# Both expert tables in one, with 8 KB rows gathered once per expert

## What is computed

```python
def peer_ffn(x, w_q, sub_keys, u, v):
    q = (x @ w_q).reshape(B, S, PEER_HEADS, 2, PEER_DK // 2)
    s = jnp.einsum('bshcd,cnd->bshcn', q, sub_keys)
    sv, si = lax.top_k(s, PEER_TOPK)
    ...
    best_s, pos = lax.top_k(cand_s, PEER_TOPK)
    e_idx = jnp.take_along_axis(cand_i, pos, axis=-1)
    gate = jax.nn.softmax(best_s, axis=-1)
    ...
        hid = jax.nn.gelu(jnp.einsum('td,ted->te', xt, u[et]), approximate=False)
        return jnp.einsum('te,ted->td', gt * hid, v[et])
```

## Time and profile before

| | |
|---|---|
| timed, median of 3 | 1822.17 us (1818.75 to 1827.27) |
| profiled execution, span from first to last instruction | 1995.1 us |
| PE, DVE, ACT, POOL busy | 1482.2, 1007.4, 342.9, 1016.4 us |
| gather queue | 536.94 MB, 71.5% of 16 DMA engines |

### The profile page before, as it was taken

One profiled execution on the slowest core, in us unless ns is written; L12 is line 12 of the kernel. 1 busy time (PEld: TensorE's weight loads), 2 busy tenths in 40 slices (PEclk: granted clock), 3 DMA queues, 4 the chain that ended last, 5 costly groups with the idle time before them and its releaser, 6 DMA issues.

```text
span 1995.1 us, 18642 instructions
## 1 busy us (share of the span) xinstructions
PE 1482.2 (74%) x4236; PEld 720.2 (36%) x4236; DVE 1007.4 (50%) x2400; ACT 342.9 (17%) x921; POOL 1016.4 (51%) x1197
## 2 busy tenths in 40 slices
PE   7997467777666877766889974577776777777677
PEld 5775233344322422222345552244432222222223
DVE  0226766666664544444122267666666645434442
ACT  1222111111111111111123221111110211111111
POOL 1111556655566466666400005555555666666663
PEclk8998688888898989999988887988888999998999
DMA  7764998999899799999812228989997999999996
GB/s 167 153 142 158 327 372 328 331 340 331 329 356 371 281 358 367 375 366 369 300 49 57 54 78 323 352 323 342 336 337 303 364 371 378 362 359 365 361 372 259
DMA packets 236447, 591.86 MB, mean 297 GB/s; under 512 B 59136, under 2 KB 100736, under 8 KB 236416
## 3 DMA queue, kind: packets, MB, share of 16 engines
q0 software_dynamic: 147456, 536.94, 71.5%
q1 hardware_dynamic: 88960, 54.57, 10.5%
HBM read 590.37 MB, written 1.05 MB: 296 GB/s over the span
## 4 chain that ended last, share of the span: by engine, by line
PE 22%; DVE 22%; issue 19%; POOL 13%; DMA 9%; another core or an unknown queue 5%; DVEq 3%; ACT 2%; POOLq 2%; SPq 1%; ACTq 1%
DVE u_rows L1124 9%; POOL v_rows L446 6%; POOL u_rows L439 6%; PE att L671 6%; DMA v_rows<-in_peer_v_dram,idx_v 5%; PE y L554 3%; DMA u_rows<-in_peer_u_dram,idx_u 3%; PE b_qk L565 3%; PE b_vo L574 1%; ACT shared L924 1%; PE att L527 1%; PE att L524 1%; DVE hit L1094 1%; DVE hit L1090 1%
## 5 line engine op out<-in xcount | busy, mean ns | idle before, releaser
L1124 DVE CUSTOM_DVE_ANT_0 u_rows<-y,u_rows 128x1024 f32<-128x1024 f32 x512 | 615.4, 1222 | 460.0 <-DMA u_rows<-in_peer_u_dram,idx_u 412.9
L446 POOL DMA_INDIRECT v_rows<-in_peer_v_dram,idx_v x512 | 483.8, 945 | 319.6 <-issue 147.0
L671 PE MATMUL att<-v_rows,shared 128*128 128x512 f32 x1024 | 510.8, 631 | 172.9 <-DMA v_rows<-in_peer_v_dram,idx_v 131.4
L439 POOL DMA_INDIRECT u_rows<-in_peer_u_dram,idx_u x512 | 485.6, 948 | 240.2 <-issue 158.6
L671 PE MATMUL y<-v_rows,shared 128*128 128x512 f32 x1024 | 493.1, 630 | 81.4 <-DMA v_rows<-in_peer_v_dram,idx_v 52.6
L671 PEld LDWEIGHTS att<-v_rows,shared 128*128 128x128 f32 x1024 | 184.3, 196 | 498.7 <-issue 454.3
L671 PEld LDWEIGHTS y<-v_rows,shared 128*128 128x128 f32 x1024 | 197.4, 202 | 368.3 <-issue 360.0
L646 PE MATMUL b_vo<-keysT,qT 128*128 128x128 f32 x128 | 28.4, 359 | 199.6 <-ACT qT L908 136.1
L924 ACT ACTIVATE shared<-ident,wts 128x128 f32<-128x128 f32 x512 | 154.2, 387 | 65.7 <-PE att L671 38.3
L919 ACT ACTIVATE act_hid<-hid 128x16 f32<-128x16 f32 x32 | 6.9, 216 | 819.9 <-issue 446.2
L632 PE MATMUL b_qk<-hT,w_pq 128*128 128x256 f32 x448 | 103.8, 392 | 3.8 <-DMA w_pq<-in_peer_w_q_dram 3.8
(11 more groups left out here) (158 smaller groups left out, 1068.1 us busy)
## 6 DMA issues: line engine op xcount, KB each, us to landing
w_pq<-in_peer_w_q_dram SPq DMA_DIRECT2D x16, 1024.0 KB
w_qk<-in_na_w_in_dram SPq DMA_DIRECT2D x16, 512.0 KB, 5.0
u_rows<-in_peer_u_dram,idx_u POOLq DMA_INDIRECT x512
v_rows<-in_peer_v_dram,idx_v POOLq DMA_INDIRECT x512
w_v<-in_na_w_in_dram SPq DMA_DIRECT2D x8, 512.0 KB, 3.8
shared<-in_na_rel_bias_dram SPq DMA_DIRECT2D x64, 64.0 KB, 4.6
w_o<-in_na_w_out_dram SPq DMA_DIRECT2D x8, 512.0 KB, 4.0
w_o<-in_mla_w_out_dram SPq DMA_DIRECT2D x8, 512.0 KB, 3.4
```

The lines of the kernel that those rows point to most:

```text
L439: pool.indirect_dma_start(u_rows[:, b, :], None, u_table, bass.IndirectOffsetOnAxis(ap=idx_u[:, half_no, b:b + 1], axis=0))\
L446: pool.indirect_dma_start(v_rows[:, b, :], None, v_table, bass.IndirectOffsetOnAxis(ap=idx_v[:, half_no, b:b + 1], axis=0))\
L671: last = nc.tensor.matmul(ffn[tile][:, c, :], diag[:, k, :], v_rows[:, b, c * 512:(c + 1) * 512], start=False, stop=stop and k == TOPK - 1)
L1124: V.tensor_tensor_reduce(out=rows, in0=px, in1=rows, scale=1.0, scalar=0.0, op0=ALU.mult, op1=ALU.add, accum_out=hid[:, k:k + 1])\
```

## The change

- The host lays u and v of an expert side by side in one table with rows of 8 KB (peer_uv). One gather brings both halves into one of 8 slots of uv_rows. The memory in SBUF is the same as that of the two rings before. A slot is free again after the expert's product on PE.
- v is no longer one group behind. In PE's loop the order is score_step(g+1), then add_experts(g).
- Weights are made for two experts at a time (SUB = 2): ACT's Gelu, DVE's product with the gates and ACT's two diagonals follow each pair of dots; DVE's part of a pair is placed after the first dot of the next pair. gate_exp moves into weigh, behind the fourth pair. One part of the choice of groups 0 and 7 is placed at other dots.
- POOL copies 16 indices at once, where it copied 8 for u and 8 for v.

```diff
+SUB = 2
+SUBS = TOPK // SUB
...
-        u_rows = sb("u_rows", [P, RING, D])
-        v_rows = sb("v_rows", [P, RING, D])
+        idx = sb("idx", [P, 2, TOPK], i32)
+        uv_rows = sb("uv_rows", [P, RING, 2, D])
...
+            def gather_group(layer, g, slot, heads=None):
+                n = layer * GROUPS + g
                 if heads is not None:
                     pool.wait_ge(s_top[0], layer * PH + heads)
                     pool.sem_inc(s_pool, 1)
+                nc.gpsimd.tensor_copy(idx[:, slot, :], expert_flat[:, ds(g * TOPK, TOPK)]).then_inc(s_ix, 1)
+                pool.wait_ge(s_ix, n + 1)
+                pool.sem_inc(s_pool, 1)
+                for k in range(TOPK):
+                    pool.wait_ge(s_acc, products_done(n * TOPK + k + 1 - RING))
+                    pool.sem_inc(s_pool, 1)
+                    pool.indirect_dma_start(uv_rows[:, k % RING, :, :].rearrange("p h d -> p (h d)"), None, uv_table,
+                                            bass.IndirectOffsetOnAxis(ap=idx[:, slot, k:k + 1], axis=0))\
+                        .then_inc(s_rows_in[k % RING], 16)
...
                     pe.wait_ge(s_diag, (base + g) * TOPK + k + 1)
-                    pe.wait_ge(s_vg[b], 16 * ((base + g) * 2 + k // RING + 1))
...
+                add_experts(layer, 0, 0)
                 with pe.Fori(1, PH - 1) as g:
                     score_step(layer, g + 1)
-                    add_experts(layer, 0, g - 1)
+                    add_experts(layer, 0, g)
                 score_step(layer, PH)
-                add_experts(layer, 0, PH - 2)
                 add_experts(layer, 0, PH - 1, stop=True)
+                add_experts(layer, 1, PH)
...
+                for s in range(SUBS):
+                    some = slice(s * SUB, (s + 1) * SUB)
+                    act.wait_ge(s_dot, (base + g) * TOPK + (s + 1) * SUB)
+                    nc.scalar.activation(act_hid[:, some], hid[:, some], ACT.Gelu).then_inc(s_gelu, 1)
+                    act.wait_ge(s_wts, (base + g) * SUBS + s + 1)
+                    for k in range(s * SUB, (s + 1) * SUB):
+                        if not first:
+                            act.wait_ge(s_acc, products_done((base + g - 1) * TOPK + k + 1))
+                        nc.scalar.activation(diag[:, k, :], ident[:, :], ACT.Copy, scale=wts[:, k:k + 1])\
+                          .then_inc(s_diag, 1)
+                    if s == 3 and choice is not None:
+                        gate_exp(layer, choice[0], choice[1])
...
                 with act.Fori(1, PH - 1) as g:
                     store_queries(layer, g + 1)
-                    gate_exp(layer, g + 1)
-                    weigh(layer, g)
+                    weigh(layer, g, (g + 1, (0, 1)))
...
                 for k in range(TOPK):
                     dot(layer, g, k)
+                    if k % SUB == 0 and k:
+                        weights(layer, g, k // SUB - 1)
...
-                weights(layer, g)
+                weights(layer, g, SUBS - 1)
...
-                dots(layer, 0, (1, (0,), (2, 4, 6, 7)))
+                dots(layer, 0, (1, (0,), (2, 4, 6, 9)))
...
-                dots(layer, PH - 1, (PH, (1,), (5, 8, 10, 12)))
+                dots(layer, PH - 1, (PH, (1,), (4, 7, 9, 11)))
...
+    laid = {**inputs, **tables, 'peer_uv': _np.concatenate([inputs['peer_u'], inputs['peer_v']], axis=-1)}
```

More of the change, by code:

```diff
@@ L208, in program @@
         s_ix = sem("indices_copied")
-        s_ug = [sem(f"u_rows_landed{i}") for i in range(RING)]
-        s_vg = [sem(f"v_rows_landed{i}") for i in range(RING)]
+        s_rows_in = [sem(f"expert_rows_landed{i}") for i in range(RING)]
         s_dot = sem("dot_done"); s_gelu = sem("gelu_done"); s_wts = sem("weights_ready")
@@ L231, in choice_no @@
             return step + 1
-        def dots_done(n):
-            return n + RING
         def products_done(n):
@@ L456, in gathers @@
+            def gathers(layer):
+                gather_group(layer, 0, 0, heads=1)
+                gather_group(layer, 1, 1, heads=2)
+                with pool.Fori(1, PH // 2) as m:
+                    for e in range(2):
+                        gather_group(layer, 2 * m + e, e, heads=2 * m + e + 1)
                 pool.wait_ge(s_top[1], (layer + 1) * PH)
                 pool.sem_inc(s_pool, 1)
-                with pool.Fori(PH, GROUPS) as g:
-                    gather_group(layer, g, start + 4 * g - 2)
@@ L460, in gathers @@
-                gather_group(layer, GROUPS, start + 4 * GROUPS - 2, with_u=False)
+                with pool.Fori(PH // 2, GROUPS // 2) as m:
+                    for e in range(2):
+                        gather_group(layer, 2 * m + e, e)
             hr = ROPE // 2
@@ L713, in peer @@
                     latents_transposed(0)
-                with pe.Fori(PH + 1, GROUPS) as g:
-                    add_experts(layer, 1, g - 1)
+                with pe.Fori(PH + 1, GROUPS - 1) as g:
+                    add_experts(layer, 1, g)
                 add_experts(layer, 1, GROUPS - 1, stop=True)
@@ L913, in gate_exp, with weigh @@
                 nc.scalar.activation(best_e[:, some, :], best_d[:, some, :], ACT.Exp).then_inc(s_be, 1)
-            def weigh(layer, g, first=False):
+            def weigh(layer, g, choice=None, first=False):
                 base = layer * GROUPS
-                act.wait_ge(s_dot, dots_done((base + g + 1) * TOPK))
-                nc.scalar.activation(act_hid[:, :], hid[:, :], ACT.Gelu).then_inc(s_gelu, 1)
-                act.wait_ge(s_wts, base + g + 1)
-                for k in range(TOPK):
-                    if not first:
-                        act.wait_ge(s_acc, products_done((base + g - 1) * TOPK + k + 1))
-                    nc.scalar.activation(diag[:, k, :], ident[:, :], ACT.Copy, scale=wts[:, k:k + 1])\
-                      .then_inc(s_diag, 1)
+                for s in range(SUBS):
[10 more added lines that the diff above has]
+                        gate_exp(layer, choice[0], choice[1])
             def peer(layer):
@@ L939, in peer @@
                 store_queries(layer, 1)
-                gate_exp(layer, 1, (0,))
-                weigh(layer, 0, first=layer == 0)
+                weigh(layer, 0, (1, (0,)), first=layer == 0)
                 with act.Fori(1, PH - 1) as g:
                     store_queries(layer, g + 1)
-                    gate_exp(layer, g + 1)
-                    weigh(layer, g)
-                gate_exp(layer, PH, (1,))
-                weigh(layer, PH - 1)
+                    weigh(layer, g, (g + 1, (0, 1)))
+                weigh(layer, PH - 1, (PH, (1,)))
                 weigh(layer, PH)
@@ L1128, in _, with weights @@
             gate_flat = gate[:, :, :].rearrange("p t n -> p (t n)")
-            def weights(layer, g):
-                dve.wait_ge(s_gelu, layer * GROUPS + g + 1)
-                V.tensor_tensor(wts[:, :], act_hid[:, :], gate_flat[:, ds(g * TOPK, TOPK)], ALU.mult)\
+            def weights(layer, g, s):
+                dve.wait_ge(s_gelu, (layer * GROUPS + g) * SUBS + s + 1)
+                some = slice(s * SUB, (s + 1) * SUB)
+                V.tensor_tensor(wts[:, some], act_hid[:, some], gate_flat[:, ds(g * TOPK + s * SUB, SUB)], ALU.mult)\
                  .then_inc(s_wts, 1)
@@ L1279 @@
     for name in _INS + list(tables):
-        a = _np.ascontiguousarray(tables[name] if name in tables else inputs[name])
+        a = _np.ascontiguousarray(laid[name])
         arrays[f"in_{name}_dram"] = a
```

49 lines of the change are left out of this document (7 added, 42 removed).

## The result

The changed kernel takes **1854.8 us** (1851.6 to 1860.5), the kernel before 1820.9 beside it: ratio **1.018** (95% 1.015 to 1.021), slower by 34 us where I had said 99. The profiled span is 1855.8. In two of the six sets of runs of the experiments the kernel before took 1982 to 2006 us, in the other four about 1821 (medians 1820 to 1824); the longer time is also that of its first profile (span 1995.1), and the variants of the changed kernel that ran beside it in those two sets took 1803 to 1856. So the trials are compared with the changed kernel's 1855, and where rows of before are needed they come from a second profile of it with a span of 1818.2.

A forecast was written before the change was run, and what follows sets the result against it. DMA at 410 GB/s was taken to bound tile 1, waits round PE, ACT and DVE tile 0's loop. Per layer 40 + 322 + 361 + 8 + 5 = 736; adjusted +50 over 702: 1822 + 2 x 50 = 1922, said 1920; range 1855 to 1980.

The forecast's parts named there:

- The chain: Tile 0 loop: PE, ACT and DVE wait for each other in turn; 1885 to 1960 us, chance 0.62.
- s: Unexplained 12.4 us wait before ACT's query copy, at most 6 timed; staying in full gives 1960 to 1990, chance 0.10.
- the ring: Tile 0 loop: PE's query products, ACT's copy, DVE's dots and choice, PE's last products in sequence; 51.7 us before clock surcharge.
- 53.7 + s: Length of a tile 0 loop group after the change: 51.7 us, 2 for PE's clock, plus the unexplained copy wait.
- The DMA is the limit: Tile 1: transfers at 2.56 us an expert set the pace, POOL's 2.48 being 3% from it.
- Removed cost: nothing, since DMA hides it: POOL: halving the number of gathers saves no time, as POOL's work lies under the transfers; 0 us.
- the 13 us of "lower rate": Per layer, kernel before: timed 702 us against 689 worked at 410 GB/s, read as slower transfers or copy wait.
- bigger rows are faster: Rival: transfers at 2.42 us an expert win 20 us a layer; 1888, or 1870 with further gains; chance 0.10.
- I see no reason for either end, and take +50: Layer slowdown between +43 and +66 us, 1908 to 1954 in all; +50 taken, giving 1922.
- 702 us a layer: Kernel before, timed: (1822 - 417) / 2, the time of one layer.
- Group 0 at 40: Start of a layer: group 0 needs both halves, 16 x 2.56 us, about 40 us instead of 30.
- The ends, -24: Behind the loop of a layer: 361 us instead of 373, tail 5 instead of 17; -24 us.

The follow-up runs named there:

- e1: Changed kernel with ACT's copy of the queries moved from ahead of a group's first pair to behind it: 1816.5 us, ratio 0.9955 to the kernel before.
- the doubled numbers: Changed kernel with DVE's three passes turning positions into expert numbers done twice in the loop of tile 0: 1900.1 us.
- e3: Changed kernel with u and v in their own tables again, two gathers of 4 KB rows for an expert: 1879.7 us.
- e6: Changed kernel with weights made for four experts at a time instead of two: 2036.5 us.
- e8: Changed kernel, tile 1 scores and split query products behind products 7 to 11, copy ahead of pair 7's Gelu, choice in nine parts: 1803.2 us.
- e12: Changed kernel, query products behind products 1, 3, 5, 7, tile 1 scores behind 9, choice in nine parts: 1852.6 us.

## Why the prediction was wrong, and where it was right

**The chain was the right one.** DVE stops before its first weights, ended by ACT; ACT stops ahead of the copy, ended by PE; the DMA share is 0.91 in the loop and 1.01 in tile 1; POOL's time halves; the 30 us of products at the end are gone. Moving the copy alone gives the whole loss back (e1), and the doubled numbers show that DVE's choice lies in the chain at full price. Two of the prediction's own signs went against it all the same: a loop group is 51.1 us, where 60 or more was to show it and under 52 was to refute it, and the share in the loop is 0.91, not under 0.8. Both signs were worked out with the 12.4 us of s in the profile, which isn't there. The trials that opened it show what I had not seen: the way of the eight slots is nearly as long, 47 to 51 us by the trials' groups, so opening the ring gives back 4 us a group and not 7.

**The steps that failed** are sizes, and one premise. The first is the length of the ring, "53.7 + s". Its terms, forecast and then measured in the rows above:
- key scores and query products 7.5; 7.55 (348.19 to 355.74)
- copy, table load, Gelu 2.3; 0.83 (to 356.57). No table load stands there: the two loads stand around the choice's exponential (375.47 and 377.01 in ACT's timeline), and ACT waits 3.87 us for DVE behind them.
- DVE until the weights of pair 4: 27.4; 25.55 (to 382.12). In the chain the weights cost 0.07 to 0.16 us each and not 0.25, and the third part of the choice 5.2, not 6.1: I took 422.36 to 428.48 as work, and a break of 0.74 us was in it.
- to the first product 0.7; 0.72
- products 8 to 15: 13.8 and 2 for the clock; 16.5. The surcharge was right, a little short: behind PE's 3.9 us break the granted clock is 0.50 from 383 to 387 us, the 1.2 GHz level, 0.85 in the next four and 1.00 from 391 on.

The sum is 51.14, 2.6 less, with s = 0: over twelve groups 31 us. Group 1 of a layer, shorter still (48.5 and 46.6), adds some 7.

**"The DMA is the limit"**, and so "Removed cost: nothing, since DMA hides it". This is the premise that failed. The prediction had POOL 3% under the pace of tile 1, from 2 x 1.24 us an expert, and left out the copies of indices, 1 us more for every eight experts. With them POOL needs 2.61 us an expert, and in the kernel before that is the pace. One gather an expert takes this limit away. Taken for bigger rows were 3 to 4 us a layer; e3 measures 25 us in both layers. An expert takes 2.50 us (39.9 a group) from 2.61 (41.8), and e3 stands between with 41.0.

Behind the loop the layers took 386.7 and 368.2 us, on average 10 less than the 387 that my terms give with the 13 us of "lower rate" in them; 4 were foreseen, so 12 us more in the two layers. The 13 us were carried over to the changed kernel as if they were the transfers'; some 7 of them were POOL's (an estimate: nine groups behind the loop at 41.8 us instead of 41.0), and the change removes these. (PE's cycle without s, told as 39.5 us, sums to 39.1, which changes nothing.) The rival "bigger rows are faster" priced them at 20 us a layer with a chance of 0.10: as far above the 12 to 13 that e3 measures as my 4 are below. Its mechanism isn't shown, for e3 changes the rows and POOL's work together. The Trainium skill, DMA: Bandwidth & Descriptors, "Rules for kernel authors", asks for at least 1 MiB in a DMA. The runs agree in direction, with several gathers in flight: those of 1 MB sustain 420 GB/s in tile 1, those of half of it 410 in e3.

**"I see no reason for either end, and take +50".** There was one: the lower end (+43) has the 13 us as a lower rate, the upper (+66) as s = 6. The second profile of before has waits of 4.0 us ahead of the copy that cost nothing, so s = 0, and 404 to 406 GB/s. That is 14 us more. 31 + 7 + 12 + 14 makes 64, and 1920 was 65 too high; group 0, 1 us longer than its 40 in each layer, takes 2 of the 64 back.

**What held.** 702 us a layer for the kernel before: 708.8 and 693.1. Group 0 at 40: 41.3 and 40.7. The ends, -24: -29 and -35 with the rate. The ring of eight slots holds in tile 1, and with weights by four (e6) it doesn't. s, to which I gave 0.10, isn't in any profile of the changed kernel.

What s is stays open. It stood in one profile of three of the kernel before and in none of the others, and no view names it. Open is also why the choice in nine parts gains 46 us in one order, nothing in another and loses 19 in a third.

The fastest is e8 at 1803.2, then e1 at 1816.5. e1 is 0.45% faster than the kernel before beside it. e8 was measured where before took 1993.9; against before's usual 1821 it would be 1% faster, which no run shows side by side.

## What to carry to other kernels

When one engine's result starts to be needed earlier, look at what is queued ahead of it on the engine that makes it: here one copy, harmless in the old order, tied three engines into a ring, and moving it by one pair undid the loss. Sum such a ring from the rows, leave out what a row doesn't place in it, and sum the next chain too, for that is where the gain of opening it ends. Add up what the issuing engine does for a whole group, its small copies too, before you say that the transfers hide it: here 3% of apparent slack was none. And take a second profile before you work out terms: a wait that no view can explain may not be there in the runs that are timed.

## What the runs showed of the hardware

- One packet carries an 8 KB row (65536 rows a launch; the queue's packets fall by 73728), and POOL's cost of an indirect DMA of 128 rows is 0.94 to 0.96 us for 4 KB and for 8 KB rows.
- In tile 1 of the kernel before and of e3, POOL issues a gather every 1.24 us when nothing holds it up (0.94 busy, 0.30 between). For 128 rows of 4 KB that is 422 GB/s, before the copies of indices are counted. Sustained rates into one core: in tile 1 404 and 410 GB/s with gathers of 4 KB rows, at which POOL has at most 1% of its time left, and 420 with 8 KB rows, at which it has about half.
- The DMA share reads 1.02 where POOL's issuing sets the pace, as it reads 1.01 where POOL waits for slots and DVE for landings: a full share doesn't tell the two apart.
- The same kernel took 1821 us in five sets of runs and 1994 in two, on chip numbers where it had taken 1821 before; the variants with the changed gathers beside it there took 1803 to 1856.
- A 1 MB load of query weights beside full gathers takes 16.5 us from issue to landing in the second profile of before (median, 300 to 450 us), and in e12 26 us stand in the chain for it.
